# Layer changes by token tile, with the RMS factor applied after the products

## What is computed

```python
def rms_norm(x, g):
    y = x32 * lax.rsqrt(jnp.mean(x32 * x32, axis=-1, keepdims=True) + NORM_EPS)
    return (y * g.astype(jnp.float32)).astype(x.dtype)

def swiglu(h, w_gate, w_up, w_down):
    return (jax.nn.silu(h @ w_gate) * (h @ w_up)) @ w_down

for layer in range(DEPTH):                       # 2
    x = x + 0.5 * swiglu(rms_norm(x, ffn_pre_norm[layer]), ...)
    h = rms_norm(x, mix_norm[layer])
    if layer % 2 == 0:
        x = x + mla_sgu_mixer(h, ...)            # latent attention and spatial gating
    else:
        x = x + short_conv_mixer(h, ...)         # (b * conv3(c * z)) @ w_out, b, c, z = split(h @ w_in)
    x = x + 0.5 * swiglu(rms_norm(x, ffn_post_norm[layer]), ...)
return rms_norm(x, final_norm)
```

## Time and profile before

| | |
|---|---|
| median of 3 runs | 1937.73 us (1935.63 to 1943.02) |
| profiled execution | 1938.75 us, span 1937.0 us |
| TensorE products | 1851.6 us busy, 96% of the span |
| TensorE weight loads | 1721.5 us, 89% |
| VectorE | 1052.9 us, 54% |
| ScalarE | 851.6 us, 44% |
| granted TensorE clock, mean | 0.983 |

### The profile page before, as it was taken

The page is one execution under the profiler, slowest core; times in us unless marked ns, Lnnn a source line. Parts: engine busy times, 40 slices in busy tenths (PEclk is TensorE's granted clock), DMA queues, the critical chain, the costliest instruction groups (busy, mean ns, idle before and its releaser), DMA issues.

```text
span 1937.0 us, 31040 instructions
## 1 busy us (share of the span) xinstructions
PE 1851.6 (96%) x12912; PEld 1721.5 (89%) x12912; DVE 1052.9 (54%) x1033; ACT 851.6 (44%) x885; POOL 91.1 (5%) x123
## 2 busy tenths in 40 slices
PE   6998899999998899999999998999999999989998
PEld 6996799999886799999899988799989998979997
DVE  4764656555754655555744455454555455655444
ACT  4454443434554443343443466434353435344343
POOL 7000011000300011000000000000000000000000
PEclk9998999999999999999999999999999999999999
DMA  7532456555431556555555534165546554646552
GB/s 223 174 131 86 164 168 212 183 185 195 153 131 44 174 173 199 192 179 190 158 183 185 185 115 151 54 207 184 184 136 212 181 188 134 215 131 195 176 193 87
DMA packets 236856, 320.12 MB, mean 165 GB/s; under 512 B 5537, under 2 KB 210704, under 8 KB 236528
## 3 DMA queue, kind: packets, MB, share of 16 engines
q1 hardware_dynamic: 234080, 309.09, 49.4%
q0 software_dynamic: 2704, 10.00, 1.6%
HBM read 317.98 MB, written 1.08 MB: 165 GB/s over the span
## 4 chain that ended last, share of the span: by engine, by line
PE 87%; DVE 6%; ACT 4%; DMA 2%; issue 1%; SPq 0%; DVEq 0%; ACTq 0%
PE PB L320 19%; PE PB L321 19%; PE PB L322 19%; PE Y L320 9%; PE Y L321 9%; PE Y L322 9%; PE Y L530 1%; ACT HI L791 1%; DVE LO L1213 1%; DMA gate_scratch<-SM 1%; PE PB L382 1%; DVE ST L1276 1%; DMA AR<-gate_scratch 1%; DVE XN L1273 0%; ACT XN L852 0%
## 5 line engine op out<-in xcount | busy, mean ns | idle before, releaser
L1213 DVE TENSOR_TENSOR LO<-RAW,HI 128x2048 fp32r<-128x2048 f32 (+1 forms) x297 | 676.5, 2280 | 535.6 <-ACT HI L791 535.6
L320 PE MATMUL PB<-XTH,HI 128*128 128x256 f32 x2896 | 822.5, 284 | 9.7 <-DVE XTL L1251 6.7
L321 PE MATMUL PB<-XTL,HI 128*128 128x256 f32 x2896 | 819.4, 283 | 0.0
L322 PE MATMUL PB<-XTH,LO 128*128 128x256 f32 x2896 | 819.4, 283 | 0.0
L791 ACT ACTIVATE HI<-RAW 128x2048 fp32r<-128x2048 f32 (+1 forms) x297 | 556.9, 1879 | 313.6 <-PE PB L322 257.4
L320 PEld LDWEIGHTS PB<-XTH,HI 128*128 128x128 f32 x2896 | 555.4, 192 | 16.5 <-DVE XTL L1251 7.9
L321 PEld LDWEIGHTS PB<-XTL,HI 128*128 128x128 f32 x2896 | 555.5, 192 | 2.5
L322 PEld LDWEIGHTS PB<-XTH,LO 128*128 128x128 f32 x2896 | 555.5, 192 | 0.0
L320 PE MATMUL Y<-HI,HH 128*128 128x512 f32 x560 | 221.0, 395 | 9.6 <-DVE HL L1222 9.6
L321 PE MATMUL Y<-LO,HH 128*128 128x512 f32 x560 | 220.3, 393 | 0.0
L322 PE MATMUL Y<-HI,HL 128*128 128x512 f32 x560 | 219.5, 392 | 0.0
(11 more groups left out here) (324 smaller groups left out, 1461.6 us busy)
## 6 DMA issues: line engine op xcount, KB each, us to landing
RAW<-in_w_gate SPq DMA_DIRECT2D x32, 1024.0 KB, 5.5
RAW<-in_w_up SPq DMA_DIRECT2D x32, 1024.0 KB, 5.4
RAW<-in_w_down SPq DMA_DIRECT2D x32, 1024.0 KB, 5.0
RAW<-in_ffn_pre_w_gate SPq DMA_DIRECT2D x22, 1024.0 KB, 5.3
RAW<-in_ffn_pre_w_up SPq DMA_DIRECT2D x22, 1024.0 KB, 5.3
RAW<-in_ffn_pre_w_down SPq DMA_DIRECT2D x22, 1024.0 KB, 4.9
RAW<-in_ffn_post_w_gate SPq DMA_DIRECT2D x22, 1024.0 KB, 5.3
RAW<-in_ffn_post_w_up SPq DMA_DIRECT2D x22, 1024.0 KB, 5.3
```

Of the source, the lines that this page charges most:

```text
L320: pe.matmul(out_ap, ah, bh, start=start, stop=False)
L321: pe.matmul(out_ap, ah, bl, start=False, stop=False)
L322: return pe.matmul(out_ap, al, bh, start=False, stop=stop)
L1213: dve.tensor_tensor(LO[:, slot, 0:w], RAW[:, slot, 0:w], HI[:, slot, 0:w].bitcast(F32), ALU.subtract).then_inc(s["w_split"], 1)
```

## The change

1. **Residual in halves.** `residual_tile` writes X in two halves of 512 columns, each with a signal (`x_sum`). The last layer norm of the first block does the same.
2. **Transposes of X, not XN.** `turn_rows(t)` transposes X of a tile as it is. For tile 0 it stands inside the last down unit (`ahead`), before the last quarter of its products. The chunks go to banks 1, 2, 3 and the first half of Y of tile 0, in the order of TURN. The unread products are gone at R1 to R5; at R0 the 32 stay.
3. **XTH and XTL by chunk and tile**: 16 pieces of 128 columns on each of ScalarE and VectorE, in place of 8 of 256. ScalarE waits before a bank's second chunk until VectorE is through with its first.
4. **First unit by tile.** `cols_T_by_tile` has 96 products of 128 columns (2 tiles x 2 halves x 8 chunks x 3), with tile 1's transposes between them, a half of X each. At R1 `cols_N(by_tile=True)` keeps 48 products of 256 columns, in the order tile 0, transposes of tile 1, tile 1.
5. **The row factor comes later.** The factor r of a token is a column of ST; the diagonal matrix RDG = r * I times a matrix of ones gives a tile RBC with r along the row, by two products in the middle of the up unit (`row_factors`), copied by ScalarE. VectorE multiplies each gate product by RBC into SG (`by_rows`), ScalarE applies Silu in place. The up product keeps its missing factor r; it goes into the residual's scale (ST column 11, r times 0.5). At R1 the 7 evacuations of ScalarE are cut in two, with r as their scale. At R4 the factor squared is put on one of the three parts (CSB, made by VectorE, formerly ScalarE), and r into the residual.
6. **Order.** Squares and roots stand behind XTH of both tiles on ScalarE. One `split` moves ahead of the layer change on ScalarE; on VectorE one LO stands behind the low parts, one behind the reciprocals.

```diff
+            def turn_rows(t, halves=(0, 1)):
+
+                for h in halves:
+                    if t == 0:
+                        for b in ((1, 2), (3,))[h]:
+                            claim(b, counted=False)
+                    pe.wait_ge(s["x_sum"], n.next("xs"))
+                    for c in range(4 * h, 4 * h + 4):
+                        mm = pe.transpose(turned(c), X[:, t, c * P:(c + 1) * P], IDENT[:, :])
+                    mm.then_inc(s["tp_full"], 1)
+
+            def cols_T_by_tile(bank):
+
+                slot = unit()
+                for t in range(NT):
+                    for j in range(2):
+                        for k in TURN:
+                            if j == 0:
+                                fresh_column()
+                            w = slice(k * UC + j * P, k * UC + j * P + P)
+                            x = slice(t * P, (t + 1) * P)
+                            mm = split_product(PB[:, bank, j * S + t * P:j * S + (t + 1) * P], HI[:, slot, w], LO[:, slot, w],
+                                               XTH[:, k, x], XTL[:, k, x], k == TURN[0], k == TURN[-1])
+                        if t == 0:
+                            turn_rows(1, (j,))
+                mm.then_inc(s["w_used"], 1)
+
+            def row_factors():
+
+                pe.wait_ge(s["r_diag"], n.next("rdg"))
+                for t in range(NT):
+                    mm = pe.matmul(Y[:, 0, t * P:(t + 1) * P], ONES[:, :], RDG[:, t, :], start=True, stop=True)
+                mm.then_inc(s["r_full"], 1)
...
                     for k in range(2):
+                        if ahead and t == 1 and k == 1:
+                            turn_rows(0)
                         for h in range(2):
...
-            renewed(32)
+            keep_awake(32)
+            turn_rows(0)
             swiglu()
-            renewed()
...
-            def rms(g, then=SILU_SET):
+            def rms_deferred(g):
+
+                for t in range(NT):
+                    x0 = n.next("xt", KC) - KC
+                    for i, c in enumerate(TURN):
+                        if i % 4 == 0:
+                            act.wait_ge(s["tp_full"], n.next("tp"))
+                        if i % 4 >= 2:
+                            act.wait_ge(s["xt_ready"], x0 + i - 1)
+                        act.activation(XTH[:, c, t * P:(t + 1) * P], turned(c), ACT.Identity, bias=COLS[:, 1:2],
+                                       scale=PV[:, g + c:g + c + 1]).then_inc(s["xt_hi"], 1)
                 squares()
-                table(then)
-                scaled(g, None, XTH)
-                split(2)
+                n.next("ri", 2 * NT)
+                table(SILU_SET)
+                split()
...
+                        if first:
+                            row_factors()
+                        act.wait_ge(s["g_row"], n.next("gr") + i)
+                        act.activation(SG[:, :], SG[:, :], ACT.Silu).then_inc(s["silu"], 1)
...
+            def renew(scale, g, **kinds):
+
+                residual_tile(0, scale)
+                low_rows(0, g)
+                residual_tile(1, scale)
+                low_rows(1, g)
+                n.next("tp", 4)
+                rms_deferred(g, **kinds)
...
+                def by_rows(i=0):
+
+                    g = SG[:, :].rearrange("p (j t) -> p j t", j=2)
+                    if n.at("hm"):
+                        dve.wait_ge(s["h_mul"], n.at("hm") + i)
+                    dve.tensor_tensor(g, PB[:, 0, :].rearrange("p (j t) -> p j t", j=2), bc(RBC.unsqueeze(1), 2, S), ALU.mult)\
+                        .then_inc(s["g_row"], 1)
```

More of the change, by code:

```diff
@@ L322, in split_product, with cols_T @@
                 return pe.matmul(out_ap, al, bh, start=False, stop=stop)
-            def cols_T(bank, i=0, xh=XTH, xl=XTL, new=False):
+            def cols_T(bank, i=0, xh=XTH, xl=XTL, new=False, factors=False):
                 slot = unit(i)
                 for j in range(2):
+                    if factors and j == 1:
+                        row_factors()
                     for k in range(KC):
@@ L334, in cols_T, with cols_N @@
                 mm.then_inc(s["w_used"], 1)
-            def cols_N(bank, kc=KC, cols=UC, xh=XTH, xl=XTL, k0=0, new=False):
+            def cols_N(bank, kc=KC, cols=UC, xh=XTH, xl=XTL, k0=0, by_tile=False):
                 slot = unit()
                 for t in range(NT):
-                    for k in range(kc):
-                        if new and t == 0:
-                            fresh(k)
+                    if by_tile and t == 1:
+                        turn_rows(1)
+                    for k in TURN if by_tile else range(kc):
+                        if by_tile:
+                            fresh_column()
                         w = slice(k * cols, (k + 1) * cols)
@@ L347, in cols_N, with rows @@
                 mm.then_inc(s["w_used"], 1)
-            def rows(ah, al, k0, start, stop, i=0):
+            def rows(ah, al, k0, start, stop, i=0, ahead=False):
                 slot = unit(i)
@@ L434, in mem_outputs, with ffn @@
                 mm.then_inc(s["ao_full"], 1)
-            def ffn(chunks, peel):
+            def ffn(chunks, peel, deferred=False, ahead=False):
                 def gate_up(i=0, uses=None, first=False):
-                    if uses is None:
+                    if first:
+                        claim(0, counted=not deferred)
+                    elif deferred:
+                        pe.wait_ge(s["g_row"], n.next("gr") + i)
+                    elif uses is None:
                         claim(0)
@@ L446, in gate_up @@
                         pe.wait_ge(s["h_mul"], n.next("hm") + i)
-                    cols_T(1, i)
+                    cols_T(1, i, factors=first and deferred)
                 def down(i, start, stop):
                     pe.wait_ge(s["h_lo"], n.next("h") + i)
-                    rows(*((CTH, CTL) if stop else (HH, HL)), 0, start, stop, i)
+                    rows(*((CTH, CTL) if stop else (HH, HL)), 0, start, stop, i, ahead and stop)
                 loops = chunks - 3 - peel
@@ L471, in ffn @@
                 n.next("hm")
+                if deferred:
+                    n.next("gr")
                 down(0, False, True)
@@ L499, in moe, with swiglu @@
                     pass
-            def swiglu(peel=0):
-                for _ in ffn(D_FF // UC, peel):
+            def swiglu(peel=0, ahead=True):
+                for _ in ffn(D_FF // UC, peel, True, ahead):
                     pass
@@ L899, in hidden @@
                         used()
+                        if not gated or not more:
+                            split()
                     elif down:
                         split(1, i)
-                gate()
+                gate(first=True)
                 up()
@@ L1384, in hidden @@
                         split(1, i)
+                if not gated:
+                    dve.wait_ge(s["r_row"], n.next("rrow"))
                 gate()
@@ L1824, in _ @@
             mixer_out()
-            residual(1.0)
-            rms(70 + 40)
+            renew(None, 70 + 40)
             ffn(D_FF // UC, 1)
-            residual(0.5)
+            for t in range(NT):
+                residual_tile(t, None)
             dve.wait_ge(s["fin_in"], 16)
             for t in range(NT):
-                inverse(t)
+                dve.wait_ge(s["n_act"], n.next("na"))
+                after(dve.reciprocal(ST[:, t, 15:16], ST[:, t, 14:15]))
                 dve.scalar_tensor_tensor(out=XN[:, t, :], in0=X[:, t, :], scalar=ST[:, t, 15:16], in1=LNG[:, :],
```

185 lines of the change are left out of this document (119 added, 66 removed).

## The result

The kernel takes 1949.64 us (median of five runs, 1945.15 to 1951.86) against 1937.73 (1935.63 to 1943.02) before: a ratio of 1.0052 [1.0037, 1.0066], so it is half a per cent slower. The medians are 11.9 us apart; the ratio, which is taken over all runs, makes 10.1. The forecast was 1947.5 in a range of 1936 to 1957. The profiled execution has 1949.64 us with a span of 1947.7, so 1.94 around it, and a mean granted clock of 0.984, against 0.983.

A forecast was written before the change was run, and what follows sets the result against it. TensorE, busy 96% of the span, was taken as the bound, so added work counts in full. Terms 5.4 + 5.5 + 0.5 - 1.75 + 0.15 = +9.8 us on 1937.7 gave 1947.5, range 1936 to 1957.

The forecast's parts named there:

- R1: Second block's second norm: first unit keeps 256 columns, second unit starts 2.15 us earlier; net gain 1.75 us.
- R0: Second block's first norm, behind a layer norm: rotation's preparation joins the chain, down comes later; 5.4 us lost.
- R4: Second block's fifth norm, at the convolution: no Silu or down unit in the chain; 0.45 us lost.
- The early start: At R2: rows end at 3.36, tile 0's products follow, 0.111 us each; unit ends at 15.45, 0.1 later.
- Rival 1: First unit's narrow products run at their width, 128 columns in 0.06 us: +2.8, 1940.5 us; 0.20 together with cheaper columns.
- The chain to HL: At R2, ScalarE and VectorE work up to HL: TensorE waits 1.4 us, down starts at 34.56; 1.85 lost.
- rival 2: At the layer changes: first product at 3.4 instead of 9.0, nothing behind waits; about 30 us gained, 1908; chance 0.07.
- rival 3: Clock falls around the layer changes: a low stretch costs 1.7 us, one to five make 1949 to 1956; chance 0.14.
- R2, R3 and R5: Second block's norms ahead of an ffn: each loses 1.85 us by the wait for HL, 5.5 us together.
- the end: After the last residual: the residual in halves costs 0.15 us.
- Rival 4: On ScalarE and VectorE a 128-column piece costs what 256 columns did: +18.8, 1956.5 us; chance 0.11.

The follow-up runs named there:

- experiment 2: Kernel before, with the second unit (not the first) at R0, R2, R3, R4 and R5 in 96 products of 128 columns: 1961.98 us, ratio 1.0122.
- experiment 3: Changed kernel, with HH and HL of each swiglu's first chunk ordered ahead of the second gate's row factor, Silu and split: 1938.4 us, ratio 1.0008.
- experiment 8: experiment 6 with the first unit and its columns by tile (128 columns, 96 products) as in the changed kernel: 1936.05 us, ratio 0.9999.
- experiment 5: Changed kernel, but first unit at R0 and R2 to R5 is 48 products of 256 columns after both tiles: 1934.01 us, ratio 0.9981.
- experiment 6: experiment 5 joined with the orders of experiment 3 and experiment 4, splits ahead of squares and reciprocals: 1923.89 us, ratio 0.9931.
- experiment 4: Changed kernel, with the rotation's preparation on VectorE moved from R0 to ahead of the first block's last layer norm: 1943.01 us, ratio 1.0028.
- experiment 1: Kernel before, with only the first unit at R0 and R2 to R5 in 96 products of 128 columns: 2013.49 us, ratio 1.0399.
- experiment 9: experiment 5 with its first unit at R0 and R2 to R5 in 96 products of 128 columns after both tiles: 2001.49 us, ratio 1.0326.

## Why the prediction was right

**The early start.** Rows end at 3.3 (forecast 3.36), narrow products step by 0.111 (0.111), the unit ends at 15.01 (15.45). XTH is through and the squares start at 11.4 (12.0), since the pieces are a few per cent cheaper. The product was priced by its weight load of 128 columns, from the rows of 160 columns, and experiment 2 confirms the price without anything of the change around it: 4.9 a unit. That it is the load which sets it is argued, not shown by itself. For it speaks the first narrow product behind wide ones, whose step is 0.06 (1248.06 to 1248.12), the price by width. 5.6 us were won at the start; the unit ends 0.3 earlier than before, so 5.3 were given back in it, 4.9 by the narrow products and the rest among tile 1's transposes and the waits for pieces. *Rival 1*, narrow products at their width, is refuted. The Trainium skill (TensorE: Matmul & The Clock Gate, Back-to-back issue gap) has about 81 ns for pairs of load and product of 128 columns; the streams shown here step by 0.11 at the full clock, and the measurement decides.

**The chain to HL.** Forecast 34.56, measured 34.61, a gap of 1.95 (1.90 at R3, 1.86 at R5). LO of up starts at 11.8 (12.4). The wait came out longer than the 1.4 of the forecast because TensorE was through sooner, at 32.8 instead of 33.2, and HL was not. The terms were right; what the prediction did not see is how free the order was. It took the queue of ScalarE and VectorE as given, while experiment 3 takes the whole wait ahead of down away by exchanging two calls. This also shows what *rival 2* lacked: its early first product is there, but with the wait removed (experiments 3 and 8) the kernel is only where it was before. What the early start wins, the narrow unit takes.

**R0.** 5.26 later at down, forecast 5.4. The stretch lost 6.85, since behind the wait of 2.5 the granted clock is 0.50 for 3.4 us, and half of that is lost. This is *rival 3* at one place, at the price of 1.7 that it named. In turn the low stretch of the kernel before at 930 to 934 is gone; the granted clock is 1.00 from 926.5 to 938.5. Both executions with a wait of 2.5 ahead of down at R0 have the half-speed stretch (the changed kernel and experiment 5). None without that wait has it (experiments 3, 6 and 8), nor has experiment 4, where it is 1.86 and the wait ahead of the second gate unit is gone as well. At R2, R3 and R5, with waits of 1.9, there is none either. So the stretch goes with the long wait; how long a wait it takes, and whether the earlier one has a part in it, is not shown.

**R1.** The second unit starts at 12.92 where it was 15.31, 2.4 earlier (forecast 2.15), but only 0.63 of it reached R2. In the attention part the changed kernel's execution ran at 0.72 over 18 us where the one before had 0.91. The change is not needed for that: experiment 2, whose code from R1 to R2 is that of the kernel before, also has 0.72 there, and takes 123.79 from R1 to R2 against 121.68. Like against like, the change wins 2.7 (121.05 against 123.79, both at 0.72) or 2.9 (118.75 in experiment 3 against 121.68, both at 0.91), where the forecast had 1.75. The term was right in mechanism and a little small, and a difference in clock between single executions took most of the gain back in this pair. Why the clock is lower there in one execution and not in another is open.

**R4.** +1.45 for 0.5. Over 20 us at the convolution's end the granted clock was 0.83 and had been 0.91, which would be up to 1.7 us; whether that is the change's doing or the execution's is not settled. Experiments 3 and 4 have about the same loss (1.7 and 1.6) and the same mean clock in the stretch, 0.97. Experiment 8, with the tile order too and with 0.98 as before, loses only 0.4. Experiment 1, which has nothing of the change, spends as long at the low clock there (0.50 over 6.8 us). This speaks for the execution and against the change, but experiment 8 differs in its order as well, so it stays open.

**R2, R3 and R5** lost 5.76 for 5.5, and the end 0.21 for 0.15. *Rival 4* is refuted by the 455 and 351 ns. The three stretches that were mis-sized, each with a lower granted clock in it, are R0 by 1.5, R1 by 1.1 and R4 by 1.0, most of the 3.8 us between the sum of 9.8 and the 13.6 of the stretches; by the medians the kernels differ by 11.9. That the sum comes so near the 10.7 of the profiled pair is partly luck: the untouched start happened to be 2.94 shorter, which hides part of the 13.6. An estimate without the clock at R1 and R4: less 2.1 (experiment 2 against before) and less 1.1 (changed kernel against experiment 8), the seven stretches make 10.4, near the 9.8 of the sum and the 10.1 of the ratio.

**Where the expected gain is.** Experiments 5 and 6 show it: transposing X at once and applying the factor later is worth having, with 256 columns in the first unit; the token tile order of the five narrow units is what costs, 12 us between experiments 8 and 6. R1, whose unit stays at 256 columns, keeps the tile order in all of them and gains. At R2 experiment 6 has its first product 2.7 us earlier than before (6.27 against 8.97), pays 0.4 for the row factor's products and has down 1.9 earlier (30.83 against 32.75). What the orders of experiment 6 would give the kernel before by themselves was not run; it has no wait ahead of its second unit or of down at R2 that they could take away. For experiment 5 by itself the place of the gain is not firm: behind R0 its profiled execution is 1.4 us longer than that of before, though its median is 3.5 lower. Its execution also had the lower clock from R1 to R2, 0.94 in the mean where before had 0.97. Experiment 6 has 12.7 us less behind R0 (1006.4 against 1019.05).

## What to carry to other kernels

An earlier start by half the tokens halves the width of the products; before it is made, hold what is won against the price of the narrow ones, which here was 0.111 us for 128 columns, nearly that of 256. When a chain of two engines ends just as TensorE asks for it, look first at what stands in their queues ahead of the piece that is asked for and is needed later: that order cost 8.5 to 11 us here, and exchanging two calls mends it. Price a changed stretch together with the stretch in front of it: here the same 96 products cost nearly twice as much behind the pause of a layer change as behind dense products. And before a stretch of a single execution is put down to the change, look for the same clock in a kernel that lacks the change.

## What the runs showed that was not expected

The same stream of 96 products of 128 columns runs at 2.4 GHz straight behind dense products of 256 or 512 columns (granted clock 1.00 in experiment 2 and at R2 to R5 of the changed kernel) and at 1.2 GHz behind the pauses and transposes of a layer change (0.51 and 0.50 in experiments 1 and 9), though TensorE is busy throughout. At R0 of the changed kernel it kept 1.00 behind 8 transposes and a wait of 0.8 us, so the line between the two is not drawn here. In the kernel before, the unit of 256 columns behind the pause of R2 kept 1.00 (1250.4 to 1256.8). The same unit in experiment 2 fell to 0.51 as well, but for 3.4 us only. In the narrow streams the clock, once low, stayed there for 20.5 to 23.9 us, about the length of 96 products 0.213 apart. Half of that is lost at each of five places, 53 us together, and experiments 1 and 2 differ by 2013.49 - 1961.98 = 51.5. I had expected experiment 1 at +22 to +24 us. What in the narrow stream keeps the clock down was not tried.
